# The first S5 stage of a four-layer block kernel: another order, output powers on GpSimd, one gate block summed on VectorE

## The reference, cut to what matters

```python
c_act = jax.nn.silu(c)
shift1, scale1, gate1, shift2, scale2, gate2 = jnp.split(c_act @ ada_w[l] + ada_b[l], 6, axis=-1)
h = modulate(rms_norm(x, norm1_g[l]), shift1, scale1)      # h * (1 + scale) + shift
...
def s5_mixer(h, ...):
    dt = jnp.exp(log_dt)[:, None]
    ab = exp(lr * dt) * (cos(li * dt) + i sin(li * dt))      # 64 groups x 64 states, complex
    bb = f(ab, lam) * b                                      # (groups, states, 16), complex
    # s[t] = ab * s[t-1] + bb @ u[t];  y[t] = Re(c @ s[t]) + d_skip * u[t]
    g = jax.nn.gelu(y)
    return g * jax.nn.sigmoid(g @ w_glu + b_glu)
...
x = x + gate1 * mix
h = modulate(rms_norm(x, norm2_g[l]), shift2, scale2)
x = x + gate2 * swiglu(h, ffn_w_gate[l], ffn_w_up[l], ffn_w_down[l])
```

## Time and profile before

| | us |
|---|---|
| median of 3 runs | 1229.67 (1226.98 to 1230.12) |
| the profiled execution, its own time | 1233.93 |
| its span, first to last instruction | 1231.7 |
| first matmuls of the GLU's last part start | 135.14 |
| first full matmuls of the FFN start | 163.27 |
| PE busy / DVE busy / POOL busy | 1164.1 / 480.4 / 52.5 |

### The profile page before, as it was taken

How to read it: one execution, slowest core, us unless ns; L and a number is a source line. 1 busy time by engine, 2 the same in 40 slices (tenths; PEclk the granted TensorE clock), 3 DMA queues, 4 the chain that set the end, 5 groups by cost and what they waited for, 6 DMA issues and landing times.

```text
span 1231.7 us, 19272 instructions
## 1 busy us (share of the span) xinstructions
PE 1164.1 (95%) x8403; PEld 960.1 (78%) x8403; DVE 480.4 (39%) x950; ACT 283.2 (23%) x674; POOL 52.5 (4%) x73
## 2 busy tenths in 40 slices
PE   5876999999999999999999999999999999999997
PEld 3535788888887867688888888788899767886666
DVE  6896264441313428623000000427364542405431
ACT  4521330000002445612000000233122322004431
POOL 2310001110000000000000000000022000000000
PEclk9987999999999899999999999999999999999989
DMA  9969669987643234163535341544410004543210
GB/s 301 367 184 354 216 224 378 357 332 268 250 161 110 103 120 139 36 211 110 192 109 198 104 169 35 164 137 138 134 57 4 3 1 137 196 146 103 66 37 35
DMA packets 120770, 196.68 MB, mean 160 GB/s; under 512 B 5772, under 2 KB 104750, under 8 KB 113262
## 3 DMA queue, kind: packets, MB, share of 16 engines
q1 hardware_dynamic: 110554, 132.20, 33.2%
q0 software_dynamic: 8336, 59.77, 12.7%
q10 hardware_dynamic: 1796, 3.47, 0.9%
HBM read 192.54 MB, written 1.05 MB: 157 GB/s over the span
## 4 chain that ended last, share of the span: by engine, by line
PE 86%; DVE 6%; DMA 3%; ACT 3%; issue 1%; POOL 0%; SPq 0%; DVEq 0%; ACTq 0%
PE psum L624 64%; PE psum L955 12%; PE psum L872 2%; PE psum L1391 2%; ACT arena L2371 2%; DMA ring<-in_ada_w 2%; DMA aring<-in_ada_w 1%; DVE arena L1581 1%; DVE stat L1630 1%; PE psum L1182 1%; DVE arena L1587 1%; PE psum L851 1%; PE psum L713 1%; DVE hT L1581 1%; PE psum L1152 1%
## 5 line engine op out<-in xcount | busy, mean ns | idle before, releaser
L624 PE MATMUL psum<-hT,ring 128*128 128x256 f32 x1392 | 313.2, 382 | 2.9 <-ACT hT L2371 1.8
L624 PEld LDWEIGHTS psum<-hT,ring 128*128 128x128 f32 x1392 | 263.3, 191 | 43.4 <-issue 7.3
L2371 ACT ACTIVATE arena<-psum 128x256 f32<-128x256 f32 (+5 forms) x215 | 96.9, 476 | 654.4 <-PE psum L624 596.0
L624 PE MATMUL psum<-hT,arena 128*128 128x256 f32 (+1 forms) x960 | 162.8, 337 | 2.7 <-DVE hT L1581 2.5
L624 PEld LDWEIGHTS psum<-hT,arena 128*128 128x128 f32 (+1 forms) x960 | 141.4, 176 | 22.9 <-issue 4.2
L1581 DVE TENSOR_TENSOR arena<-arena,psum 128x256 f32<-128x256 f32 (+1 forms) x75 | 39.2, 536 | 296.4 <-ACT arena L2371 267.2
L624 PE MATMUL psum<-arena 64*64 64x64 f32 (+6 forms) x1996 | 111.3, 247 | 2.3 <-issue 1.9
L624 PEld LDWEIGHTS psum<-arena 64*64 64x64 f32 (+4 forms) x1996 | 89.4, 140 | 18.6 <-issue 15.6
L624 PE MATMUL psum<-ring,arena 128*128 128x256 f32 (+2 forms) x320 | 85.8, 433 | 0.5 <-ACT arena L2371 0.5
L955 PE MATMUL psum<-arena,ring 128*128 128x256 f32 x384 | 85.1, 380 | 0.0
L1587 DVE SCALAR_TENSOR_TENSOR acc<-aring,c_act,acc 128x2048 f32<-128x2048 f32 x28 | 65.8, 2349 | 43.8 <-DMA aring<-in_ada_w 25.4
(11 more groups left out here) (232 smaller groups left out, 1120.7 us busy)
## 6 DMA issues: line engine op xcount, KB each, us to landing
aring<-in_ada_w POOLq DMA_DIRECT2D x32, 1024.0 KB, 7.6
ring<-in_ada_w POOLq DMA_DIRECT2D x16, 1024.0 KB, 14.9
ring<-in_a_w_in SPq DMA_DIRECT2D x14, 1024.0 KB, 5.4
arena<-in_ffn_w_gate SPq DMA_DIRECT2D x12, 1024.0 KB, 8.2
arena<-in_ffn_w_up SPq DMA_DIRECT2D x12, 1024.0 KB, 8.3
ring<-in_ffn_w_down SPq DMA_DIRECT2D x12, 1024.0 KB, 5.0
ring<-in_ffn_w_gate SPq DMA_DIRECT2D x10, 1024.0 KB, 9.5
ring<-in_ffn_w_up SPq DMA_DIRECT2D x10, 1024.0 KB, 6.6
```

The source lines that it names most:

```text
L624: return eng.matmul(dst, w, x, start=first, stop=last)
L2371: return eng.activation(dst, x, f, **k)
```

## The change

EARLY and WIDE fall from 24 to 16: PE multiplies blocks 0 and 1 only. Block 2 is summed by DVE directly behind the scan, into a new area acc_early, over the two aring slots. All output powers go to POOL, among its panel loads: (block 0, imaginary) and (0, real) during input_powers, the others behind the second "u_ready". DVE keeps three of seven toep memsets, POOL does four at its start. U is modulated in two halves, each with a "u_ready". inputs() goes by halves, wT has three areas, the toeplitz copies go in two halves, xT is turned from xC_in, so the second load of x goes. Five matmuls of ones (keep_warm) stand ahead of the transposes of c.

```diff
-EARLY = 24
-WIDE = 24
+EARLY = 16
+WIDE = 16
...
# PE
+            keep_warm(5, "s")
...
+            ada_panels(9, 3)
             chunk_inputs(0)
+            inputs(3, 0)
             chunk_inputs(1)
...
+            ada_panels(12, 1)
+            inputs(3, 1)
+            kernel_rows(3)
             chunk_inputs(2)
...
+            kernel_columns(1)
             chunk_inputs(3)
-            kernel_columns(0)
-            kernel_columns(1)
+            ada_panels(13, 1)
             vector_columns(1, "s")
             vector_columns(2, "s")
-            ada_panels(11, 5)
+            ada_panels(14, 2)
...
             glu_part(2, glu_w[2][0], range(4))
+            ada_rows(2, "s")
             gelu_columns(1)
+            row_columns(2, row_of[2], "s")
...
# SP
             for i in range(2):
                 sp.wait_ge(*emptied_at(("kernT", i)))
...
+                for t in range(L5 - 1):
+                    n = P5 * (t + 1)
+                    sp.dma_start(toep[P - n:P, t, 512 * i:512 * i + 512], toep[0:n, L5 - 1, 512 * i:512 * i + 512])\
+                      .then_inc(done(f"toeplitz{i}_landed"), 16)
...
# DVE
             for i in range(4):
                 eng.wait_ge(*emptied_at(("U", i)))
...
+            modulate(0)
+            input_powers(3, (1,))
+            modulate(1)
...
-            output_powers(0)
...
-                if u < 6 * BJ // 2:
...
-            output_powers(2)
-            output_powers(3)
             ada_bias(1)
-            ada_bias(2)
...
+            for i in range(KC):
+                ada_panel()
...
# POOL
+            def output_powers(b, i, temp, loads=(0, 0, 0)):
...
+                for n, (to, pw, co) in enumerate(((dst, powr, ct[:, i]), (temp, powi, ct[:, 1 - i]))):
+                    G.tensor_tensor(to, pw[:, k9, js].rearrange("p k j -> p j k").unsqueeze(3).to_broadcast([P, BJ, L5, P5]),
+                                    co[:, js, :].unsqueeze(2).to_broadcast([P, BJ, L5, P5]), ALU.mult).then_inc(*g.step())
+                    ada_loads(loads[n])
+                eng.wait_ge(*g.last)
+                G.tensor_tensor(dst, dst, temp, (ALU.add, ALU.subtract)[i]).then_inc(*g.signals("ca_ready"))
+                ada_loads(loads[2])
...
+            output_powers(0, 1, ahead, (0, 1, 1))
+            eng.wait_ge(done("xc_scaled"), 8)
...
+            output_powers(0, 0, ahead, (0, 1, 1))
+            ada_loads(3)
+            eng.wait_ge(done("u_ready"), 2)
+            output_powers(1, 0, behind, (1, 0, 0))
+            output_powers(1, 1, behind)
+            eng.wait_ge(*filled_at(("bu", 2)))
+            output_powers(2, 0, behind)
+            eng.wait_ge(*filled_at(("kernT", 1)))
+            output_powers(2, 1, behind)
+            ada_loads(1)
+            output_powers(3, 0, behind, (1, 1, 1))
+            output_powers(3, 1, behind, (1, 1, 0))
```

More of the change, by code:

```diff
@@ L665, in coefficient_columns, with keep_warm @@
                     last.then_inc(*fills(("raw", m, h)))
+            def keep_warm(n, pool="a"):
+                b = POOLS[pool][turns[pool] % len(POOLS[pool])]
+                eng.wait_ge(emptied[b], bank_uses[b])
+                for _ in range(n):
+                    mm(psum[:, b, 0:T], ones, const_sb[:, 0:T])
             eng.wait_ge(done("b_landed"), 16 * 2)
@@ L741, in kernel_columns @@
                 for x in range(4):
-                    last = eng.matmul(ps[:, x * P:(x + 1) * P], kern[:, 4 * i + x, :], ident, start=False, stop=True,
+                    last = eng.matmul(ps[:, x * P:(x + 1) * P], kern[i][:, x, :], ident, start=False, stop=True,
                                       skip_group_check=True)
@@ L763, in _ @@
             ada_panels(0, 2)
+            eng.wait_ge(done("xc_landed"), 16 * 4)
+            for h in range(2):
+                for y in range(2):
+                    key = ("xT", h, y)
+                    eng.wait_ge(*next_bank(key, "b"))
+                    ps = bank_of(key).rearrange("p (s n) -> p s n", n=P)
+                    for x in range(4):
+                        last = eng.transpose(ps[:, x, :], xC_in[:, 4 * y + x, h * P:(h + 1) * P], ident)
+                    last.then_inc(*fills(key))
+            ada_panels(2, 1)
+            inputs(0, 0)
+            eng.wait_ge(done("const5_landed"), 16)
+            eng.wait_ge(done("xc_squares"), 8)
+            eng.wait_ge(*next_bank("xstat", "s"))
+            mm(bank_of("xstat")[:, 0:L5], con5("same_chunk"), ss[:, 0, :]).then_inc(*fills("xstat"))
+            inputs(0, 1)
+            kernel_rows(0)
+            ada_panels(3, 1)
             eng.wait_ge(done("group_rows_ready"), 1)
@@ L829, in own_inputs @@
                                    skip_group_check=True)
-            ada_panels(16, 4)
-            eng.wait_ge(done("toeplitz_clear"), 7)
-            eng.wait_ge(done("toeplitz_landed"), 16 * 7)
+            eng.wait_ge(done("toeplitz_clear"), L5 - 1)
             for i in range(2):
                 eng.wait_ge(*emptied_at(("kernT", i)))
-            for i in range(4):
-                own_inputs(i // 2, i % 2)
-            ada_panels(20, 4)
-            row_columns(2, row_of[2], "s")
+                eng.wait_ge(done(f"toeplitz{i}_landed"), 16 * (L5 - 1))
+                for r in range(2):
+                    own_inputs(i, r)
             def state_outputs(b):
                 eng.wait_ge(done("states_ready"), 1)
-                eng.wait_ge(done("ca_ready"), 2 * (b + 1) + (BJ - 2 if b else 0))
+                eng.wait_ge(done("ca_ready"), 2 * (b + 1))
                 kh = b // 2
@@ L898, in _ @@
                 glu_part(i, glu_w[i][0], range(4, 8) if i < 3 else range(8))
-            def keep_warm(n, pool="a"):
-                b = POOLS[pool][turns[pool] % len(POOLS[pool])]
-                eng.wait_ge(emptied[b], bank_uses[b])
-                for _ in range(n):
-                    mm(psum[:, b, 0:T], ones, const_sb[:, 0:T])
             def mean_square(key, chunks, src, sig, count, pool="a"):
@@ L1634, in _ @@
             V.memset(rows[:, :], 0.0).then_inc(*v.signals("rows_clear"))
+            for t in range(3):
+                V.memset(toep[0:P - P5 * (t + 1), t, :], 0.0).then_inc(*v.signals("toeplitz_clear"))
             def vector_columns(i):
@@ L1737, in input_powers @@
                     eng.wait_ge(done("ab_taken"), 1)
-                elif b == 3:
+                elif b == 3 and 0 in parts:
                     eng.wait_ge(*filled_at(("kern", 0)))
@@ L1842, in _ @@
                           bank_of(key).rearrange("p (t k c) -> p t k c", t=4, k=4)).then_inc(*v.empties(key))
+            ada_bias(2)
+            eng.wait_ge(*v.last)
+            modulation(0, 0, 4, cols("norm2_g", 0, KC))
             V.tensor_copy(raw_h[:, :, T], ada_cols(0, 3)).then_inc(*v.signals("raw_shift"))
@@ L2459, in take_gelu_columns @@
                     bank_of(key).rearrange("p (t k c) -> p t k c", t=4, k=4), ACT.Copy).then_inc(*s.empties(key))
-            take_inputs(0)
+            take_x(0, 0)
+            for i in range(2):
+                take_inputs(0, i)
             eng.wait_ge(done("xc_rstd"), 1)
@@ L2498, in _ @@
             take_gelu(1)
+            take_row(2, row_of[2])
             take_gelu_columns(2)
@@ L2895, in _ @@
             G.memset(c_half, 0.0).then_inc(*g.signals("halves_clear"))
+            for t in range(3, L5 - 1):
+                G.memset(toep[0:P - P5 * (t + 1), t, :], 0.0).then_inc(*g.signals("toeplitz_clear"))
             eng.wait_ge(done("b_landed"), 16 * 2)
@@ new lines, in _, with ada_loads @@
+            begun = [10]
+            def ada_loads(n):
+                for _ in range(n):
+                    ada_load(begun[0])
+                    begun[0] += 1
+            ahead, behind = sq[:, 1024:2048], tmp5[:, 0:1024]
+            for h in range(2):
+                eng.wait_ge(*emptied_at(("raw", 1, h)))
+            eng.wait_ge(done("xc_squares"), 8)
+            eng.wait_ge(*filled_at("xstat"))
+            eng.wait_ge(*filled_at("grp"))
+            output_powers(0, 1, ahead, (0, 1, 1))
```

195 lines of the change are left out of this document (83 added, 112 removed).

## The result

The changed kernel takes 1251.74 us (median of four runs, 1248.99 to 1253.67) against 1229.7 us: a ratio of 1.0182, with a 95% interval of 1.0155 to 1.021. It is slower by 22 us, where 29 had been forecast. Its profiled execution took 1253.43 us, with a span of 1251.6.

A forecast was written before the change was run, and what follows sets the result against it. Behind the first stage the kernel was taken as a PE chain, so the GLU's last part sets the change's worth: 135.14 to 164.5, 29 us on 1229.67 gives 1258.7. Predicted 1258, range 1217 to 1266.

The forecast's parts named there:

- the disputed term: POOL and DVE products both reading two SBUF tiles: cost between nothing and one waiting for the other in full; 0.50.
- The front: DVE ahead of the scan: U's end at 55.9; at the upper end six POOL products add 13.7 us, scan starts 80.1.
- turns: DVE and POOL products wait for each other in full: GLU's last part 29 us later, total 1258.7; chance 0.50.
- The scan: DVE's 30 steps: eleven meet a POOL product and last 2.66 us instead of 0.73, so it ends at 123.2.
- Behind it: After the scan: load 18 to last product 21.5 us plus 7 to 10 of hold-ups; ca_ready about 154, GLU's last part 164.5.
- the order without turns: New order with no contention: GLU's last part at 124 instead of 135.14, a gain of 11 us.
- The total: Shift of the GLU's last part, 29 us, added to the median 1229.67; PE's FFN was to shift with that row.
- Rival B: Whole kernel: no contention between POOL and DVE, 1229.67 - 11 = 1218.7, range 1214 to 1226; chance 0.24.
- the toeplitz chain: Copies ahead of PE's local outputs at 101.36, latest of three chains; with the change in place at 85, ahead of the scan.

The follow-up runs named there:

- memset_all: Changed kernel with each of POOL's 24 products replaced by two memsets of 1024 columns, output powers left out: 1220.92 us, ratio 0.9934 to the kernel before.
- before_memsets: Kernel before with 16 POOL memsets of 1024 columns added beside its scan, two in place of each product: 1229.08 us, ratio 1.0002.
- before_products: Kernel before with eight POOL products of 1024 columns added beside its scan: 1232.15 us, ratio 1.0019.
- rearranged_sbuf: rearranged_panels with the four step factors back in SBUF, and without the wait for their bank: 1231.93 us, ratio 1.0025 to the kernel before.
- third_tensor: Changed kernel with the third gate block (panels 16 to 23) given back to PE: 1243.95 us, ratio 1.0118 to the kernel before.
- rearranged_panels: Changed kernel with third gate block on PE, step factors in PSUM, some powers on DVE, loads earlier, row columns later: 1211.62 us, ratio 0.9858 to the kernel before.

## Why the prediction was right, point by point

**The kind of contention** was the disputed term, taken at its upper end, at even odds. The runs confirm the mechanism from both sides: it goes with POOL's reads (memsets) and with DVE's second SBUF operand (an operand in PSUM), and stays with one read of POOL. By the Trainium skill (SBUF — State Buffer, "Who interferes with whom") a VectorE instruction with two SBUF inputs contends with a GpSimd instruction that reads SBUF; the trace agrees, 2.38 us for 0.29, 0.29 with an operand in PSUM, 0.64 beside a copy.

**The front.** u's end was forecast at 55.9 without and 69.6 with turns; it came at 57.57 (memset_all) and 67.28. So the turns cost 9.7 us here and not 13.7: DVE was already part of the way through an instruction when POOL's began, and once POOL waited instead. The scan's start with turns, 80.1, was 80.74, but that hit is luck: without turns it was to be 66.4 and was 72.58, 6.2 us late, and the turns moved it by 8.2 us, 5.5 less than reckoned.

**The scan.** Eleven long steps were forecast and eleven came, but at 2.28 us each ((106.50 - 81.47) / 11 in DVE's rows), not 2.66: a step's reduction and hand-overs run beside POOL's product, so it costs the step 1.55 us, not 1.93. The scan ended at 119.67, not 123.2.

**Behind it.** The last product was to be ready at 154; PE went on at 148.20. From load 18 (121.25) to the last product's end (148.05) it was 26.8 us: 5.3 more than the 21.5 without meetings, where 7 to 10 had been added. From 148.20 to the GLU's last part 11.5 us passed, where 10 to 11 had been reckoned. The row came at 159.68, not 164.5: 3.5 us are the scan's, the meetings behind it gave 2 to 3, and the last stretch took 1 back. Against the order without turns the row was to move by 40.5 us (124 to 164.5) and moved by 30.8 (128.89 to 159.68). The contention was priced a third too high and the order alone 4.9 us too low; in part these two errors cancel.

**The total.** FFN rows moved as that row did: the first full matmuls from 163.27 to 187.82, 24.55 us. The spans differ by 19.9 only. Of the difference 3 us are given back in one place, 32 matmuls far behind the first stage. The stretches in the kernel before, and (second) in the changed one:

```profile
410.00:421.00 11.00, 11.00 (x39) 9.32 (x39) 0.00 (x0) 1.41 (x9) 0.00 (x0) 0.70 0.54 191
```
```profile
434.00:443.00 9.00, 9.00 (x48) 8.04 (x48) 0.31 (x3) 1.84 (x11) 0.00 (x0) 1.00 0.64 234
```

They took 10.07 us in the profiled execution of before, 8.84 in before_memsets, 7.15 in before_products and in the changed kernel, with granted clocks of 0.70, 0.84, 1.00 and 1.00. Since the same instructions give all three, this belongs to the execution and not to the change. Some 1.7 us more go in the same way near 790 us (16 matmuls in 4.93 us before, in 3.62 in the changed kernel). Both slow stretches lie in the profiled execution of before, which is 4.3 us above its median; the medians differ by 22.0. A shift read between two profiles has an error of this size.

**Rival B** was right in its sum, 1218.7 against 1220.92 measured without turns, but not in its steps. The scan was to begin at 66.4 and began at 72.58. The step that failed is PE's: it was to be free for the first chunk input at 50, to reach chunk input 2 at 59 and to have 7.4 us to go to the scan. Its transposes and three panels held it until 54.39, so it got to chunk input 2 at 62.4, and had 10.2 us to go: a wait of 1.16, and slower matmuls at a granted clock of 0.86 from 60 to 72 us (chunk input 3 took 2.79 us, not 2.06). The GLU's last part came at 128.89, not 124; that the total is nearer to B's than this row is, lies within the error just named.

**What was not seen:** that the old order had 13.3 us of slack in its scan. The new order takes away the toeplitz chain that gave it. It is the same edit that would have made the gain and that laid the scan bare: the eight products in the old order cost some 3 us, if anything, twelve in rearranged_sbuf cost 20 us.

## What to carry to other kernels

Before work goes to GpSimd beside VectorE, count on both sides the SBUF tiles that each instruction reads: if VectorE's reads two and GpSimd's reads any, nearly every GpSimd instruction holds one VectorE instruction for what is left of its own length. In a chain of short ones that was 1.55 us a step beside products of 2.0 to 2.4 us, and 0.35 us beside copies of 1.04. Cures, in order of ease: put one operand of the short instruction into PSUM (one operand moved was worth 15 to 20 us here), or run the two in each other's idle time. And read the slack of the chain that is to be disturbed before pricing the disturbance; a change that also shortens the neighbouring chain spends that slack.

## What the runs showed of the hardware that was not expected

A POOL load between two products does not always let VectorE in. DVE, then POOL, in rearranged_sbuf:

```profile
70.74 5.51 DVE L1592 TENSOR_TENSOR sq<-stat,arena 128x128 f32<-128x128 f32 x1
```
```profile
70.94 2.04 POOL L2934 TENSOR_TENSOR arena<-arena,acc 128x1024 f32<-128x1024 f32 x1
72.92 1.12 POOL L2916 DMA_DIRECT2D ring<-in_ada_w  x2
74.05 2.04 POOL L2934 TENSOR_TENSOR arena<-stat,acc 128x1024 f32<-128x1024 f32 x1
```

The step's product waited over both products and the 1.12 us of issuing between them, and ended 0.16 us behind the second. By the Trainium skill (the section named above) whoever issues first holds the shared pair for the whole instruction; here it was held over two instructions and what lay between them, so the trace goes further than the rule. In third_tensor two steps lasted 4.7 us in the same way: there twelve products were met by ten long steps. In rearranged_sbuf too all twelve products fell into the scan (9 or 10 had been reckoned) and were met by ten long steps; they cost it 21.7 us (43.66 against 21.99), 1.8 each where 1.5 had been reckoned. Hardly any of that was hidden: the scan ended 17.7 us later than in rearranged_panels and the GLU came 16.6 later. So the loss was 20 us and not 8 to 12.

A copy with one input can be held as well: in third_tensor a DVE copy of 128 x 32 (f32, SBUF to SBUF) at 67.19, issued as POOL's product of 67.10 to 69.16 ran, took 2.01 us instead of 0.17. It is one instance.

The record of a held instruction begins before POOL's (81.47 and 81.66 above), so the order of the starts does not tell who waits; the ends do.

Two executions with the same instructions of PE up to the scan, rearranged_panels and rearranged_sbuf, were granted clocks of 0.68 and 1.00 from 60 to 75 us. PE's last chunk input took 3.63 us in the one and 2.06 in the other, and the scans began at 73.99 and 70.01.
